# Stick-breaking attention by section, the embedding with its projections first, and the first norm's sum on VectorE

## The reference, cut to what matters

```python
def ple_add(x, p_i, g, w_gate, w_proj):                       # "embedding"
    gate = jax.nn.sigmoid((rmsnorm(x, g) @ w_gate).astype(F32))
    return x + (gate * (p_i @ w_proj).astype(F32)).astype(x.dtype)

def sb_block(q, k, v, q_pos, k_pos):                          # stick-breaking
    z = jnp.einsum('bqhd,bkhd->bhqk', q, k) * (HD_SB ** -0.5)
    valid = (k_pos[None, :] < q_pos[:, None])[None, None]
    log_1m = jnp.where(valid, jax.nn.log_sigmoid(-z), 0.0)
    log_a = jax.nn.log_sigmoid(z) + lax.cumsum(log_1m, axis=3, reverse=True) - log_1m
    a = jnp.where(valid, jnp.exp(log_a), 0.0)
    return jnp.einsum('bhqk,bkhd->bqhd', a, v.astype(F32)).astype(q.dtype)

for i in range(2):
    x = x + 0.5 * swiglu_a(rmsnorm(x))                        # "ffn"
    x = x + (retention if i == 0 else stick_breaking)(rmsnorm(x))
    x = x + 0.5 * swiglu_b(rmsnorm(x))                        # "ffn"
    x = ple_add(x, p[i], ...)
y = rmsnorm(x)
```

## Time and profile before

| | us |
|---|---|
| median of 3 runs (2925.68 to 2931.76) | 2927.53 |
| the profiled execution | 2930.01 |
| its span, first to last instruction | 2928.5 |
| TensorE matmuls busy | 2836.9 |
| VectorE / ScalarE / GpSimd busy | 1737.2 / 1130.7 / 208.8 |
| mean granted TensorE clock (1 is 2.4 GHz, 0.5 is 1.2 GHz) | 0.985 |

### The profile page before, as it was taken

The page is one execution under the profiler, slowest core; times in us unless marked ns, Lnnn a source line. Parts: engine busy times, 40 slices in busy tenths (PEclk is TensorE's granted clock), DMA queues, the critical chain, the costliest instruction groups (busy, mean ns, idle before and its releaser), DMA issues.

```text
span 2928.5 us, 47449 instructions
## 1 busy us (share of the span) xinstructions
PE 2836.9 (97%) x19230; PEld 2782.4 (95%) x19230; DVE 1737.2 (59%) x2393; ACT 1130.7 (39%) x1438; POOL 208.8 (7%) x199
## 2 busy tenths in 40 slices
PE   7999999999999999999999999999999989999997
PEld 7999999999999999999998999999999979999996
DVE  6757464546465575756547666565545468474655
ACT  4425243323232443434434334344444444252442
POOL 2000003111011200000110000011000010000011
PEclk9999999999999999999998999999999999999998
DMA  3222223233232212222321222223222111222221
GB/s 118 80 80 87 73 80 125 92 112 120 77 133 98 78 60 89 80 87 72 96 72 54 89 75 87 79 80 117 74 85 76 65 43 65 87 80 87 74 94 51
DMA packets 68083, 246.63 MB, mean 84 GB/s; under 512 B 7952, under 2 KB 8224, under 8 KB 66880
## 3 DMA queue, kind: packets, MB, share of 16 engines
q1 hardware_dynamic: 58608, 204.67, 21.3%
q0 software_dynamic: 9296, 39.40, 3.8%
HBM read 226.74 MB, written 17.30 MB: 83 GB/s over the span
## 4 chain that ended last, share of the span: by engine, by line
PE 86%; DVE 8%; issue 2%; ACT 2%; POOL 0%; DMA 0%; POOLq 0%; DVEq 0%; ACTq 0%; SPq 0%
PE ps L426 38%; PE ps L488 30%; PE ps L749 7%; PE ps L618 4%; PE ps L794 2%; DVE w_lo L1441 1%; DVE xn L1473 1%; ACT w_hi L869 1%; DVE x_lo L1446 1%; PE ps L721 1%; PE ps L818 1%; DVE t_lo L1500 1%; PE ps L784 1%; PE ps L688 0%; PE ps L810 0%
## 5 line engine op out<-in xcount | busy, mean ns | idle before, releaser
L869 ACT ACTIVATE w_hi<-raw 128x1024 fp32r<-128x1024 f32 (+1 forms) x242 | 249.0, 1029 | 829.6 <-PE ps L426 652.3
L1441 DVE TENSOR_TENSOR w_lo<-raw,w_hi 128x1024 fp32r<-128x1024 f32 (+1 forms) x242 | 294.3, 1216 | 109.1 <-ACT w_hi L869 106.2
L426 PE MATMUL ps<-g_hi,w_hi 128*128 128x320 f32 x1408 | 320.0, 308 | 0.0
L426 PE MATMUL ps<-g_hi,w_lo 128*128 128x320 f32 x1408 | 320.0, 307 | 0.0
L426 PE MATMUL ps<-g_lo,w_hi 128*128 128x320 f32 x1408 | 319.9, 308 | 0.0
L426 PE MATMUL ps<-x_hi,w_hi 128*128 128x320 f32 x1216 | 288.7, 319 | 23.6 <-DVE x_lo L1446 19.6
L426 PE MATMUL ps<-x_lo,w_hi 128*128 128x320 f32 x1216 | 280.7, 312 | 0.0
L426 PE MATMUL ps<-x_hi,w_lo 128*128 128x320 f32 x1216 | 280.4, 312 | 0.0
L1673 DVE SCALAR_TENSOR_TENSOR x<-ps,x 128x640 f32<-128x640 f32 x96 | 79.2, 824 | 334.1 <-PE ps L426 334.1
L426 PEld LDWEIGHTS ps<-x_hi,w_hi 128*128 128x128 f32 x1216 | 206.3, 191 | 31.3 <-DVE x_lo L1446 14.2
L426 PEld LDWEIGHTS ps<-g_hi,w_hi 128*128 128x128 f32 x1408 | 234.9, 187 | 0.0
(11 more groups left out here) (260 smaller groups left out, 6564.8 us busy)
## 6 DMA issues: line engine op xcount, KB each, us to landing
raw<-wst SPq DMA_DIRECT2D x356, 512.0 KB, 3.4
raw<-wst SPq DMA_DIRECT2D x32, 384.0 KB, 2.9
s<-st_d POOLq DMA_DIRECT2D x8, 1024.0 KB, 5.2
sts_o<-s POOLq DMA_DIRECT2D x16, 512.0 KB, 3.1
rd<-dec_d POOLq DMA_DIRECT2D x8, 640.0 KB, 5.5
kc<-kc_d POOLq DMA_DIRECT2D x8, 512.0 KB, 4.4
vc<-vc_d POOLq DMA_DIRECT2D x8, 512.0 KB, 5.5
x<-xT SPq DMA_DIRECT2D x8, 320.0 KB, 6.3
```

Source lines behind the costliest of these rows:

```text
L426: last = nc.tensor.matmul(out[:, h, :], a, b[:, HALF * h:HALF * (h + 1)], start=start and q == 0, stop=stop and q == 2, skip_group_check=True)
L869: nc.scalar.activation(w_hi[:, (c["n"] + m) % 2, 0:cols], raw[:, r, 0:cols], ACT.Copy).then_inc(s_whi, 1)
L1441: tt(w_lo[:, p, 0:cols], raw[:, r, 0:cols], w_hi[:, p, 0:cols].bitcast(F), ALU.subtract).then_inc(s_wlo, 1)
```

## The change

- **Start.** ScalarE makes all eight `x_hi` first and then the squares; VectorE adds them up, GpSimd no longer does for this norm. One table load is left out.
- **Embedding.** All eight projections of `p` come first, evacuated into `proj`, then all eight gates. The sum of squares follows the third projection. In the first embedding the last gate signals its middle (`s_mid`), and the operand's parts of tiles 0 to 3 are made during its second half, 4 and 5 behind it, 6 and 7 behind their update. An ffn after an embedding takes its sum of squares behind the second slot (`ss_after` = 1).
- **Stick-breaking.** One written-out order `SB_ORDER` in place of lists and loops, with the counts worked out from it. The sums go over the high parts of both pieces first, then over the low ones, and stand between the halves of `v`. The values of both heads go into one bank, each with its own 64 columns of `bv`, heads alternating. `T` uses banks 5 and 6, `S` bank 7. The output projections are spread over sections 2, 3, 4 and the last; the last (`y`) goes in whole width over four accumulators, its first two tiles begin with the block that is ready, and `x_lo` follows one tile behind the sums.

```diff
+def _sb_order():
+    def proj(n, r):
+        return [(n, r, h) for h in range(2)]
+    def out(n, first):
+        return [("w", n, d, h) for d in range(first, first + 4) for h in range(2)]
+    order = proj("q", 0) + proj("k", 0) + proj("v", 0) + [("T", 0), ("ZA", 0), ("ZB", 0)]
+    for r in range(1, PAIRS - 1):
+        a = r - 1
+        order += proj("q", r) + proj("k", r) + [("v", r, 0), ("RA", a), ("RB", a), ("v", r, 1)]
+        order += [("S", a), ("T", r), ("A", a), ("ZA", r), ("ZB", r)]
+        order += {2: out(0, 0), 3: out(0, 4), 4: out(1, 0)}.get(r, [])
+    r, a = PAIRS - 1, PAIRS - 2
+    order += proj("q", r) + proj("k", r) + [("RA", a), ("RB", a)] + out(1, 4) + [("S", a), ("A", a), ("ZA", r), ("ZB", r)]
+    order += out(2, 0) + proj("v", r) + [("RA", r), ("RB", r)] + out(2, 4) + [("T", r), ("S", r), ("A", r)]
+    return order + [("y", d) for d in range(KT)]
...
-PLE_USES = [(_k, _d) for _f in (0, 4) for _k in "gp" for _d in range(_f, _f + 4)]
+PLE_USES = [("p", _d) for _d in range(KT)] + [("g", _d) for _d in range(KT)]
...
+                                ss_after=int(not i or phases[i - 1] == "ple"),
...                              # TensorE, ple
-                    if n == 0:
-                        sum_squares(c)
+                        if d == 2:
+                            sum_squares(c)
...                              # TensorE, stick
+                def sums(a):
+                    for src in (l_hi, l_lo):
+                        pe.wait_ge(s_lhi if src is l_hi else s_llo, CREDIT + 2 * a + 2)
+                        for piece in range(2):
...
+                def prompt_values(a):
+                    par = a % 2
+                    for b in range(4):
+                        for head in range(2):
+                            at_piece, z0 = ZB[head, b]
+                            rows = slice(HD * head, HD * (head + 1))
+                            last = nc.tensor.matmul(ps[rows, 0, b * P:SEQ], bv[:, par, b, rows],
+                                                    e[:, at_piece, z0:z0 + ZW[b]],
+                                                    start=b == 0, stop=b == 3, skip_group_check=True)
+                    last.then_inc(s_fill, 1)
+                def last_out(d, tiles):
+                    u = sb_banks(("y", d))[0] // 2
+                    slot = SB_SLOT["y", d]
+                    p = (c["n"] + slot) % 2
+                    for k in tiles:
+                        w = slice((2 * (d % 4) + k) * P, (2 * (d % 4) + k + 1) * P)
+                        last = mm3(acc(u), w_hi[:, p, w], w_lo[:, p, w], y_hi[:, 2 + k, :], y_lo[:, 2 + k, :],
+                                   k == 0, k == 1)
...
+                        if d == 0:
+                            released(("A", PAIRS - 2))
+                            pe.wait_ge(s_att, CREDIT + 2 * PAIRS)
+                            last_out(0, (0,))
+                            last_out(1, (0,))
+                            released(("A", PAIRS - 1))
+                        last_out(d, (1,) if d < 2 else (0, 1))
...                              # ScalarE, ple, for gate d
+                    early = d == KT - 1 and not c["last"]
+                    if early:
+                        act.wait_ge(s_mid, CREDIT + c["ple"] + 1)
+                        act.wait_ge(s_xup, CREDIT + updated(KT // 2 - 1))
+                        for k in range(KT // 2):
+                            feed_hi(to[1], k)
+                        act.wait_ge(s_fill, CREDIT + c["fill"] + n + 1)
+                        act.wait_ge(s_xup, CREDIT + updated(KT - 2))
+                        for k in range(KT // 2, KT - 2):
+                            feed_hi(to[1], k)
...                              # ScalarE, the start
-                feed(0, 0, d, s_xup, 0)
+                feed_hi(0, d)
+            for d in range(KT):
+                if d >= 2:
+                    act.wait_ge(s_ssum, CREDIT + max(2, d - 1))
+                nc.scalar.activation(sq[:, d % 2, :], x[:, d, :], ACT.Square).then_inc(s_sq, 1)
...                              # VectorE, ple
+                mean_square(c)
+                for d in range(KT):
+                    nc.vector.tensor_copy(halves(proj[:, d, :]), filled(d)).then_inc(s_free, 1)
+                    if d == 2:
+                        one_over_root(c)
+                    if d % 4 == 3:
+                        split_lo(c, ple_slot("p", d), 0, 0)
+                for d in range(KT):
...
+                    tt(halves(scr[:, d % 2, :]), filled(n), halves(rstd[:]), ALU.mult).then_inc(s_free, 1)
...
+                    tt(t, t, proj[:, d, :], ALU.mult).then_inc(s_gated, 1)
+                    dve.wait_ge(s_gated, CREDIT + count + 1)
                     tt(x[:, d, :], x[:, d, :], t, ALU.add).then_inc(s_xup, 1)
...                              # VectorE, stick, section r
+                    proj("q", r, 0)
+                    softplus(0, a)
+                    proj("q", r, 1)
+                    split(("q", r, 1))
+                    proj("k", r, 0)
+                    softplus(1, a)
+                    llo(0, a)
+                    proj("k", r, 1)
+                    llo(1, a)
+                    split(("k", r, 1))
+                    proj("v", r, 0)
+                    capped(a, 0)
+                    capped(a, 1)
+                    proj("v", r, 1)
+                    split(("v", r, 1))
+                    ylo("S", a)
+                    by_token(r)
+                    ylo("A", a)
...                              # VectorE, the start
+            for d in range(1, KT):
+                dve.wait_ge(s_sq, CREDIT + d + 1)
+                if d == 1:
+                    tt(ssum[:], sq[:, 0, :], sq[:, 1, :], ALU.add).then_inc(s_ssum, 2)
+                else:
+                    dve.wait_ge(s_ssum, CREDIT + d)
+                    tt(ssum[:], ssum[:], sq[:, d % 2, :], ALU.add).then_inc(s_ssum, 1)
```

More of the change, by code:

```diff
@@ new lines, in projection @@
+                def projection(use):
+                    kind, n, half = use[0], use[1], use[-1]
+                    slot = SB_SLOT[use]
+                    p = (c["n"] + slot) % 2
+                    if half == 0:
+                        pe.wait_ge(s_wlo, CREDIT + c["n"] + slot + 1)
+                    if kind == "w":
+                        released(("A", 2 * n + 1))
+                        blocks = [(2 * (use[2] % 4) + k, 2 * (n % 2) + k) for k in range(2)]
+                    else:
+                        blocks = [(k, k) for k in range(KT)]
+                    hi, lo = (y_hi, y_lo) if kind == "w" else (x_hi, x_lo)
+                    cols = slice(HALF * half, HALF * (half + 1))
+                    for n, (wb, xb) in enumerate(blocks):
+                        if use == ("q", 0, 0):
+                            pe.wait_ge(s_xlo, CREDIT + c["fed"] + n + 1)
+                        wh, wl = w_hi[:, p, wb * P:(wb + 1) * P], w_lo[:, p, wb * P:(wb + 1) * P]
+                        for q, (a, b) in enumerate(((wh, hi), (wh, lo), (wl, hi))):
+                            last = nc.tensor.matmul(ps[:, sb_banks(use)[0], 0:HALF], a, b[:, xb, cols],
+                                                    start=n == 0 and q == 0, stop=n == len(blocks) - 1 and q == 2)
+                    last.then_inc(s_fill, 1)
+                    if use == ("q", 0, 1):
+                        sum_squares(c)
@@ new lines, in past_logits @@
+                def past_logits(r):
+                    par = r % 2
+                    pe.wait_ge(s_kv[par], 32 * (r // 2 + 1))
+                    for s in range(STREAMS):
+                        last = nc.tensor.matmul(by_stream(zf(1)[:, Z_PAST:Z_NEW], s), kc[:, par, s, :],
+                                                bqs[:, s, :, :], start=False, stop=s == STREAMS - 1,
+                                                skip_group_check=True)
+                    last.then_inc(s_fill, 1)
@@ new lines, in stick @@
+                for d in range(4):
+                    add(2, d, 0)
+                    if d == 3:
+                        softplus(0, r)
+                    add(2, d, 1)
+                split(("w", 2, 3, 1))
+                softplus(1, r)
+                proj("v", r, 0)
+                llo(0, r)
+                proj("v", r, 1)
+                llo(1, r)
+                split(("v", r, 1))
+                capped(r, 0)
+                capped(r, 1)
+                add_four(2, 4)
+                by_token(r)
```

620 lines of the change are left out of this document (282 added, 338 removed).

## The result

The kernel before took 2927.69 us (median of 4 runs, 2925.68 to 2931.76), the changed kernel 2872.69 us (4 runs, 2871.79 to 2876.94): a ratio of 0.9815, 95% interval 0.9802 to 0.9827. That is 55.0 us less; forecast were 53.8 us less, a time of 2874 us. The profiled execution of the changed kernel took 2872.76 us with a span of 2871.2 us. Most steps came out as placed. One did not: TensorE's longest new wait stands for another cause than the one I gave.

A forecast was written before the change was run, and what follows sets the result against it. TensorE bounds the kernel, its matmuls busy for 97% of the span. The terms -10.5 - 8.4 - 17.6 - 13.2 - 5 + 0.9 sum to -53.8 us: 2876.2 us profiled, 2.5 us lower for the median, 2874 us; range 2862 to 2893.

The forecast's parts named there:

- Start: Kernel start: the first sum of squares comes at 24.4 us instead of 34.9 us, -10.5 us.
- First embedding: First embedding and next ffn's head: 12.3 us gap goes, three costs of 1.3, 0.25 and 2.3 us come, -8.4 us.
- Values: Stick-breaking prompt values: two heads of 64 columns run at once, 2.2 us gained a pair, times 8, -17.6 us.
- Waits of stick-breaking: TensorE's idle time in stick-breaking: 8.5 us instead of 21.7, -13.2 us.
- the end: Last output projections of stick-breaking: TensorE waits 3.9 us for the last x_lo, bounds 1 and 7.
- Clock: Stick-breaking's granted clock: dips that follow gaps go, those behind small matmuls stay, -5 us, bounds +10 and -9.
- Second embedding and tail: Second embedding and kernel end: fourth projection's wait costs +1.3 us, the last wait becomes 6.15 for 6.55; net +0.9 us.
- (a): Stick-breaking values: the column groups do not overlap, +17.6 us, 2892 us; chance 0.08.
- (b): Kernel start: the clock does not rise, or x lands late, +4 to +6 us, 2879 us; chance 0.13.
- (c): Stick-breaking: the soft chain is later than counted, 2 us in each of 7 sections, +14, 2888 us; chance 0.13.
- (d): Stick-breaking: clock stays at half through a pair's projections too, slower than before, about 2995 us; chance 0.02.
- (e): Whole change: start, embedding, y and values gain nothing; -5 + 0.9 are left, 2923 us, no change; chance 0.02.

The follow-up runs named there:

- the experiment: Changed kernel with the start as before: squares between the x_hi copies, their sum on GpSimd, table load back; 2882.64 us, ratio 0.9847.
- y_accumulators: Changed kernel with the last output projections in accumulators 3, 1, 0, 2, so the next ffn needs only six of eight additions; 2872.3 us, ratio 0.9812.
- full_width: Changed kernel in its new order, prompt values through all 128 columns, one head after the other, each into its own bank; 2889.98 us, ratio 0.9875.
- no_sb: Kernel before with the new start and new embeddings, stick-breaking untouched; 2914.74 us, ratio 0.9951.
- both edits together: Changed kernel with y accumulators in order 3, 1, 0, 2 and VectorE's w_lo of y 3 and y 7 behind an x_lo; 2867.86 us, ratio 0.9793.

## Why the prediction was right, and where it was not

**Start: -10.5 forecast.** The sum of squares stands at 24.86 us for 34.94, -10.1. That the experiment's medians give 10.0 is in part luck, since its trace has only 8.0 of them at the start. All eight `x_lo` take 0.88 us (median) where the earlier trace rows had 2.16. The order on ScalarE alone isn't enough: with the adds on GpSimd 6.4 of the 10 us are lost again. The adds on VectorE in the old order, and the table load by itself, were not run. Cover was thinner than I had it: the adds end at 23.7 us, not at 22.6. The clock rose at 12.6 us, not at 12.3.

**First embedding: -8.4.** From the stage's start to the end of the ffn's second slot and the sum of squares it was 98.2 us and is 88.5 us, -9.7, against -10.7 by the same steps, and +2.2 at the ffn's head for the +2.3 forecast; together -7.5. The margin of 0.2 us did not hold. The weight loads of the ffn's first projection show two stalls, ahead of the seventh block and, for the next slot's `w_lo`, ahead of the second slot:

```profile
1530.25 0.30 PEld L457 LDWEIGHTS ps<-x_hi,w_hi 128*128 128x128 f32 x2 [0.41 <-DVE x_lo L1503]
1532.53 0.30 PEld L457 LDWEIGHTS ps<-x_hi,w_hi 128*128 128x128 f32 x2 [0.40 <-DVE w_lo L1498]
```

A third stall, of 0.1 us, stands ahead of the last block. Together they cost 0.9 us, where I had 0.25 us for `w_lo` alone. My list began with a free VectorE when the last gate ends, "multiply by 1/rms to E+0.9". E is 1524.67 us in this trace, VectorE is at the `x_lo` of the first four tiles until 1525.5, and the multiply ends at 1526.22, E+1.55. The fourth projection's wait came as forecast: its first matmul starts 2.20 us behind that of the sum of squares, which has 0.83 us of work, so 1.37 us are lost for 1.3. The profile counts 0.96 of them as idle, under issue.

**Values: -17.6.** All of them took 37.7 us and take 19.0, -18.7, just past my bound of -18.6. The 3.5 of 4 that the 32-wide blocks of the earlier trace rows show was too cautious for two groups: 2.37 us a pair against 4.48 full-width is 1.9 of 2. By the Trainium skill (TensorEngine Tiling (Array Packing), Key Properties and Restrictions) a change of mode drains the array and column tiling does without fast weight loads; my estimate with that was 2.65 us a pair. If there is such a cost, it is inside the 2.37 us: here the trace doesn't agree with that estimate.

**Waits of stick-breaking: -13.2.** Idle is 4.74 us inside and 4.99 behind, 9.7 where I had 8.5, for 21.7 before: -12.0. The head, and `l_hi` in the last two sections only (1.24 and 0.96 us for 2 x 1.5), came as placed. I had not seen that the last section's stream values wait 0.95 us for `bv`. The step that failed is the one called "the end": "`x_lo` 7 is there at 24.2 us, and TensorE wants it at 14.1 + 6.2 = 20.3". The first half is exact: it is there 24.2 us behind the first `y` matmul. But TensorE did not get so far without it, since it asks for the eighth addition when the last `y` matmul is done, at 14.35 us, and that ends at 19.2 us. I had counted when each operand is ready and had not read the ffn's rule on accumulators. The sum was nearly right because the two deadlines lie close; `y_accumulators` shows that taking one away uncovers the other.

**Clock: -5.** It was -10: 12 us lost before, some 2 us after, all of them behind the wait at 2333.83. This is the mis-sized term: I let the dips behind small matmuls stand, 7 us of them, because the run `S`, `T`, `A`, `ZA`, `ZB` looked "much like now". They went: with the new order and the old widths they go (`full_width`), with the old order they stay (`no_sb`). That is outside my own bound of -9. Part of it is luck: the fall behind the 0.95 us wait, which most executions show, is missing in this one and would have cost about 1.7 us (4.06 - 2.37).

**Second embedding and tail: +0.9.** From the stage's start to the last sum of squares it was 78.2 us (2833.29 to 2911.46) and is 78.8 us (2775.38 to 2854.16), +0.6. The last wait is 5.94 us for 6.55.

By these steps: -10.1 - 7.5 - 18.7 - 12.0 - 10.2 + 0.6 = -57.9, for -57.25 between the two profiled executions (2930.01 and 2872.76); 0.65 us are in no step. The errors of the steps are +0.4, +0.9, -1.1, +1.2, -5.2 and -0.3; the largest is the clock. That the forecast of 2874 us came so near 2872.69 is in part luck, since two errors cancel: the steps sum to 3.45 us too little, and I took off 2.5 us for the median, while the changed kernel's profiled execution (2872.76) lies at its median.

**The rivals.** (a) falls with the 2.37 us pair; (b) with the matmuls every 0.147 us from 12.6 us on; (c) with two waits in two sections instead of seven; (d) with the clock of 1.00 throughout; (e) with the result.

## What to carry to other kernels

Matmuls with 64 stationary columns should alternate between the halves of the array, one by one: in turn, 1.56 of the 2.11 us that a pair gains are lost. When a stage's order changes, list for the first instruction of the next stage every semaphore that it waits on, accumulators as well as operands, and price the latest. Where the second latest is near, only both edits together pay: each alone was worth under 1 us here by the medians, the two 5.3 us.

## What the runs showed of the hardware

- Two 64-column groups overlap almost fully: 2.37 us a pair in alternation, 3.93 us in turn, 4.48 us full-width. In turn, the second head's first matmul starts 1.56 us behind the first head's, beside the first head's last two.
- VectorE's instructions with two operands in SBUF stretch beside GpSimd's adds, and GpSimd's beside them: `w_lo` 1.22 us alone and 2.59 beside, the add 1.54 and up to 2.10. The additions to `x`, with one operand in PSUM, keep their 0.81 to 0.82 us in the same stretch. The Trainium skill (GPSIMD Engine Reference, Specifications) says that they contend where a VectorE instruction has two SBUF inputs; these rows agree. The surprise was that it gave back all of the 1.3 us that a better order had won.
- The granted clock fell in the old order of small matmuls with TensorE busy throughout (0.54 in the earlier trace rows, 0.79 in `no_sb`), and does not in the new one with the same widths (`full_width`), but for once behind a wait of 0.95 us. What in the order decides is open.
- The same kernel doesn't always get the same clock in the same place: behind the same wait of 0.95 us the last pair's values took 2.37 us in one execution and 4.06 us in another; ten of twelve profiled executions show the fall there. A difference of 2 us between two profiles need not be the edit's.
